# The end of a decoder step on one core: rows of two held expert blocks normalised apart and scattered over the output, in place of three blocks whose rows are fetched back into the tiles

## The reference

```python
def rmsnorm(x, g):
    xf = x.astype(jnp.float32)
    inv = lax.rsqrt(jnp.mean(xf * xf, axis=-1, keepdims=True) + EPS)
    return (xf * inv * g.astype(jnp.float32)).astype(x.dtype)
...
    def run_block(args):
        tok, w, e = args
        xb = h[tok]
        a = jax.nn.silu(xb @ w1[e]) * (xb @ w3[e])
        return ((a @ w2[e]).astype(jnp.float32) * w[:, None]).astype(h.dtype)
...
    h2 = rmsnorm(x, g_ffn).reshape(B * L, D_MODEL)
    x = x + hier_moe(h2, w_grp, w_exp, w1, w3, w2).reshape(B, L, D_MODEL)
...
    y_prompt = rmsnorm(yp, g_final)
    y_sample = rmsnorm(ys, g_final)
```

## Time and profile before

| | us |
|---|---|
| median of 3 runs | 1014.09 |
| profiled execution | 1009.91 |
| its span, first to last instruction | 1008.2 |
| PE busy in the span | 957.0 |
| last product of block 31 on PE ends | 980.3 |
| last scaled half tile on DVE ends | 1005.0 |

### The profile page before, as it was taken

One profiled execution on the slowest core, in us unless ns is written; L12 is line 12 of the kernel. 1 busy time (PEld: TensorE's weight loads), 2 busy tenths in 40 slices (PEclk: granted clock), 3 DMA queues, 4 the chain that ended last, 5 costly groups with the idle time before them and its releaser, 6 DMA issues. The chain is left out here.

```text
span 1008.2 us, 16747 instructions
## 1 busy us (share of the span) xinstructions
PE 957.0 (95%) x5480; PEld 834.8 (83%) x5481; DVE 814.8 (81%) x1873; ACT 440.3 (44%) x736; POOL 221.5 (22%) x236
## 2 busy tenths in 40 slices
PE   6999999999999999999999999969999999999980
PEld 6998898988989889898886888858888888888870
DVE  5977877878778787787878666589999999999985
ACT  6621122121221212212114112148988988988964
POOL 0001210022100212002111110031443443444332
PEclk9999999999999999999999999979999999999995
DMA  9411106121151211611127432389999999999956
GB/s 309 160 37 59 34 31 187 32 64 32 33 186 32 64 33 33 186 32 63 54 98 248 152 142 103 112 329 407 395 393 393 392 398 387 394 395 384 364 208 248
DMA packets 77190, 191.62 MB, mean 190 GB/s; under 512 B 13808, under 2 KB 49948, under 8 KB 64691
## 3 DMA queue, kind: packets, MB, share of 16 engines
q1 hardware_dynamic: 62219, 159.10, 41.9%
q0 software_dynamic: 14752, 31.03, 10.2%
q10 hardware_dynamic: 144, 0.52, 0.2%
HBM read 172.70 MB, written 38.68 MB: 210 GB/s over the span
## 5 line engine op out<-in xcount | busy, mean ns | idle before, releaser
L1422 DVE TENSOR_TENSOR w_lo<-w,w_hi 128x1024 fp32r<-128x1024 f32 x128 | 150.5, 1217 | 0.3
L845 ACT ACTIVATE w_hi<-w 128x1024 fp32r<-128x1024 f32 x128 | 129.5, 1068 | 3.4 <-PE bank L959 3.4
L957 PE MATMUL bank<-w_hi,xT_hi 128*128 128x512 f32 x256 | 102.8, 401 | 2.4 <-issue 2.3
L2178 PE MATMUL bank<-wvg_hi,hT_hi 128*128 128x512 f32 x256 | 104.0, 406 | 0.0
L2178 PE MATMUL bank<-wvg_lo,hT_hi 128*128 128x512 f32 x256 | 101.1, 395 | 0.0
L2178 PE MATMUL bank<-wvg_hi,hT_lo 128*128 128x512 f32 x256 | 100.7, 394 | 0.0
L959 PE MATMUL bank<-w_hi,xT_lo 128*128 128x512 f32 x256 | 100.1, 391 | 0.0
L958 PE MATMUL bank<-w_lo,xT_hi 128*128 128x512 f32 x256 | 99.8, 390 | 0.0
L2581 POOL TENSOR_TENSOR mixed<-onorm,pgate 128x256 f32<-128x256 f32 x36 | 28.5, 792 | 322.2 <-DVE onorm L2353 322.2
L1981 ACT ACTIVATE v<-bank 128x256 fp32r<-128x256 f32 x32 | 12.2, 383 | 195.3 <-PE bank L2179 195.3
L957 PE MATMUL bank<-hT_hi,wuqk_hi 128*128 128x344 f32 x288 | 93.5, 325 | 0.1
(11 more groups left out here) (335 smaller groups left out, 2485.0 us busy)
## 6 DMA issues: line engine op xcount, KB each, us to landing
w<-in_w_dram SPq DMA_DIRECT2D x96, 1024.0 KB
raw<-in_w_in_dram SPq DMA_DIRECT2D x57, 256.0 KB, 3.2
mixed_d<-mixed POOLq DMA_DIRECT2D x32, 128.0 KB, 2.1
sample_state<-in_state_ret_dram SPq DMA_DIRECT2D x16, 256.0 KB, 3.4
out_dram<-sample_state SPq DMA_DIRECT2D x16, 256.0 KB, 3.8
mixed_in<-mixed_d SPq DMA_DIRECT2D x8, 512.0 KB, 4.3
x_again<-in_x_prompt_dram SPq DMA_DIRECT2D x8, 512.0 KB, 3.5
h_d<-h POOLq DMA_DIRECT2D x8, 512.0 KB, 3.0
```

What stands on the lines that cost most here:

```text
L845: act.activation(hi, whole_w, ACT.Copy).then_inc(S["up_hi"], 1)
L957: pe.matmul(out, lhs[0], rhs[0], start=first, stop=False)
L1422: dve.tensor_tensor(lo, whole_w, hi, ALU.subtract).then_inc(S["up_lo"], 1)
L2178: g = pe.matmul(gates, x[xi], wvg[wi][:, 1:3, k, :], start=first, stop=last)
```

## The change

- HELD is 2: blocks 30 and 31. Block 29 is scattered with adding, as the others are.
- SP loads all eight prompt tiles after `sum_out`. Their rows are normalised whole as they are then, without the held blocks, and stored to the output.
- POOL still writes held rows back to `sum_d`, but with `idx_sample`, in which all prompt rows lie out of bounds: only rows of sample tokens are written. Then SP loads the sample parts.
- The held rows themselves are two further entries of ORDER ("block"): squared, scaled in place in `xg`, and scattered by POOL over `y_prompt` (rows of sample tokens out of bounds) once all eight tile stores have landed.
- SP stores the samples last and waits for the scatters.
- `rows_of_held` is gone. The small tables `idx_sample` and `same_row` are made on DVE in step 2 of the loop. ACT loads the table for the root inside block 31, between the gate's sigmoid and the copy of the turned rows.
- The block of engine programs is opened with `no_gpsimd_drain=True`.

```diff
-HELD = 3
+HELD = 2
...
-        block = ctx.enter_context(nc.Block())
+        block = ctx.enter_context(nc.Block(no_gpsimd_drain=True))
...
-        AGAIN = (CH, 0, 1)
-        OVER = tuple(t for t in range(CH) if t not in AGAIN)
-        ORDER = (CH, 0, 2, 1, 3, 4, 5, 6, 7)
-        NORM_GROUPS = ((0, 2), (2, 4), (4, 6), (6, 9))
+        SUMMED = tuple(("tile", t) for t in range(CH))
+        ROWS_OF_BLOCK = tuple(("block", b) for b in range(NE - HELD, NE))
+        ORDER = (*SUMMED, *ROWS_OF_BLOCK, ("samples", 0))
+        SAMPLES = len(ORDER) - 1
+        NORM_GROUPS = ((0, 3), (3, 5), (5, 8), (8, len(ORDER)))
...
             for i in range(2):
                 sp.wait_ge(sum_out[i], SUMS[i])
-            for t in OVER:
+            for t in range(CH):
                 sp.dma_start(fin[:, t, :], sum_d[t * P:(t + 1) * P, :]).then_inc(rows_in[t], 16)
...
             sp.wait_ge(z_out, 16 * HELD)
             sp.dma_start(fin_s[:, :], in_parts(sum_d[SEQ:NTOK, :])).then_inc(rows_in[CH], 16)
-            for t in (0, 1):
-                sp.dma_start(fin[:, t, :], sum_d[t * P:(t + 1) * P, :]).then_inc(rows_in[t], 16)
-            for n, t in enumerate(ORDER):
-                dst = y_prompt[0, t * P:(t + 1) * P, :] if t < CH else in_parts(y_sample.rearrange("b o d -> (b o) d"))
-                for half in halves_of(n):
-                    sp.wait_ge(S["y_done"], after(n + 1 + half.start // 512))
-                    sp.dma_start(dst[:, half], tile_of(n)[:, half]).then_inc(y_out, 16)
-            sp.wait_ge(y_out, 16 * (NT + 1))
+            for t in range(CH):
+                sp.wait_ge(S["y_done"], after(t + 1))
+                sp.dma_start(y_prompt[0, t * P:(t + 1) * P, :], fin[:, t, :]).then_inc(y_out, 16)
+            sp.wait_ge(y_out, 16 * CH)
+            sp.wait_ge(S["y_done"], after(SAMPLES + 1))
+            sp.dma_start(in_parts(y_sample.rearrange("b o d -> (b o) d")), fin_s[:, :]).then_inc(y_out, 16)
+            sp.wait_ge(y_out, 16 * (CH + 1))
+            sp.wait_ge(z_out, 16 * 2 * HELD)
...
                         down_high(b, s % SLOTS, uses(s, g), q)
                     sigmoid(b, s % 2)
+                    sqrt_next()
                     a_high(b, s % 2)
...
                     gate(b, s % 2)
+                    many.append(spill_count(dve))
                     a_low(b, s % 2)
...
+                if isinstance(b, int) and b == 2:
+                    sample_slots()
+                    same_rows()
...
+            def sample_slots():
+
+                rows = idx_tok[:, NE - HELD:NE]
+                st.do(dve.tensor_scalar(idx_past[:, :], rows, float(SEQ), 4096.0, ALU.is_lt, ALU.mult))
+                dve.tensor_tensor(idx_sample[:, :], idx_past[:, :], rows, ALU.add).then_inc(S["rows_known"], 1)
...
-            for kind, n in TAIL:
-                if kind == "norm":
-                    a, b = NORM_GROUPS[n]
-                    dve.wait_ge(S["root_done"], after(ROOT3 + n + 1))
-                    do(rsqrt_columns(steps, dve, *(small[:, at + a:at + b] for at in (SS, MS, RS, TX))))
-                else:
+            for g, (a, b) in enumerate(NORM_GROUPS):
+                do(rsqrt_columns(steps, dve, *mean_root(g)))
+                if a == CH:
+                    dve.wait_ge(z_out, 16 * HELD)
+                for n in range(a, b):
                     scale_rows(n)
...
-            for t in OVER:
+            for t in range(CH):
                 pool.wait_ge(rows_in[t], 32)
+            pool.wait_ge(S["rows_known"], after(1))
             for i, b in enumerate(range(NE - HELD, NE)):
                 pool.wait_ge(S["z_done"], after(i + 1))
-                pool.indirect_dma_start(out=sum_d, out_offset=indexed(idx_tok[:, b:b + 1]),
+                pool.indirect_dma_start(out=sum_d, out_offset=indexed(idx_sample[:, i:i + 1]),
                                         in_=xg[b % SLOTS][:, :], in_offset=None,
                                         bounds_check=last_row, oob_is_err=False).then_inc(z_out, 16)
...
-            pool.wait_ge(S["rows_known"], after(1))
-            pool.wait_ge(z_out, 16 * HELD)
-            for t in OVER:
-                landed, count = held_in(t)
-                pool.wait_ge(landed, count - 16)
-                pool.indirect_dma_start(out=fin[:, t, :], out_offset=None, in_=sum_d,
-                                        in_offset=indexed(row_held[:, t:t + 1]),
-                                        bounds_check=last_row, oob_is_err=False).then_inc(landed, 16)
+            pool.wait_ge(y_out, 16 * CH)
+            for n, (kind, b) in enumerate(ORDER):
+                if kind == "block":
+                    pool.wait_ge(S["y_done"], after(n + 1))
+                    pool.indirect_dma_start(out=y_prompt[0], out_offset=indexed(idx_tok[:, b:b + 1]),
+                                            in_=xg[b % SLOTS][:, :], in_offset=None,
+                                            bounds_check=last_prompt, oob_is_err=False).then_inc(z_out, 16)
```

More of the change, by code:

```diff
@@ L359, in step_kernel @@
         most = rc.place("most", [P, 1], F32)
[L360 to L363, removed]
+        idx_sample = rc.place("idx_sample", [P, HELD], I32)
+        idx_past = rc.place("idx_past", [P, HELD], I32)
         assert rc.at <= whole.end
@@ L618, in down_piece, with spill_count, spilled @@
             return w2t[s][at], high_of_down(b)[:, 2 * q:2 * q + 2, :], w2_lo[s][at]
-        def spilled(eng, step, build=None, end=None):
+        def spill_count(eng):
             eng.wait_ge(S["spill_known"], after(1))
-            many = eng.value_load(spill[0:1, 2 * SPILL:2 * SPILL + 1], min_val=0, max_val=SPILL)
-            with eng.If(many > 0):
+            return eng.value_load(spill[0:1, 2 * SPILL:2 * SPILL + 1], min_val=0, max_val=SPILL)
+        def spilled(eng, step, build=None, end=None, many=None):
+            with eng.If((spill_count(eng) if many is None else many) > 0):
                 if build is not None:
@@ L880, in y_out_of_psum, with sqrt_next @@
                                    scale=slot_w[:, bass.ds(b, 1)]).then_inc(S["y_ev"], 1)
+            def sqrt_next():
+                act.activation(small[:, EPSC + 1:EPSC + 2], small[:, EPSC:EPSC + 1], ACT.Sqrt)
             def y_stored(b, s, g):
@@ L933, in more, with tiles_reloaded @@
                 y_out_of_psum(b, 0)
[L935 to L941, removed]
-                else:
[L943 to L947, removed]
+            def tiles_reloaded():
+                act.wait_ge(gains_in, GAINS + 16 * CH)
+                sqrt_next()
+            spilled(act, more, held_read, tiles_reloaded)
+            for n, (kind, i) in enumerate(ORDER):
+                if kind == "tile":
+                    act.wait_ge(rows_in[i], 32)
+                elif kind == "block":
+                    act.wait_ge(S["z_done"], after(i - (NE - HELD) + 1))
+                else:
+                    act.wait_ge(rows_in[CH], 48)
+                act.wait_ge(S["sq_done"], after(SQ3 + n))
+                act.activation(junk_f[rows_of(n), 0:tile_of(n).shape[1]], tile_of(n), ACT.Square, scale=D ** -0.5,
+                               accum_out=norm_col(SSF, n)).then_inc(S["sq_done"], 1)
+                if n == SAMPLES:
                     act.wait_ge(S["l_mm"], after(NT + 1))
-                    act.activation(small[0:SR, SS:SS + 1], banks[4][0:SR, 0:1], ACT.Copy).then_inc(S["sq_done"], 1)
+                    act.activation(norm_col(SSF, n), banks[4][0:SR, 0:1], ACT.Copy).then_inc(S["sq_done"], 1)
                 for a, b in NORM_GROUPS:
                     if b == n + 1:
-                        act.wait_ge(S["sq_done"], after(squares_before(b)))
-                        root_of_means(act, a, b).then_inc(S["root_done"], 1)
+                        act.wait_ge(S["sq_done"], after(SQ3 + b + (n == SAMPLES)))
+                        act.activation(small[:, MSF + a:MSF + b], small[:, SSF + a:SSF + b], ACT.Sqrt,
+                                       bias=small[:, EPSC:EPSC + 1]).then_inc(S["root_done"], 1)
         def three(pe, out, lhs, rhs, first, last):
@@ L1587, in more, with mean_root @@
                     down_low(b, 0, q)
[L1589 to L1606 removed]
+            spilled(dve, more, spill_list, many=many[0])
+            def mean_root(g):
+                a, b = NORM_GROUPS[g]
+                dve.wait_ge(S["root_done"], after(ROOT3 + g + 1))
+                return (small[:, at + a:at + b] for at in (SSF, MSF, RSF, TXF))
+            def scale_rows(n):
+                dve.scalar_tensor_tensor(out=tile_of(n), in0=tile_of(n), scalar=norm_col(RSF, n), in1=gain_of(n),
+                                         op0=ALU.mult, op1=ALU.mult).then_inc(S["y_done"], 1)
+            dve.wait_ge(gains_in, GAINS)
+            for g, (a, b) in enumerate(NORM_GROUPS):
[3 more added lines that the diff above has]
+                for n in range(a, b):
                     scale_rows(n)
```

79 lines of the change are left out of this document (32 added, 47 removed).

## The result

The changed kernel takes 1015.86 us (median of 14 runs) against 1012.7 us for the kernel before (14 runs): a ratio of 1.0042, 95% interval 1.0032 to 1.0052, or 3.2 to 5.3 us slower. The forecast was 1016.9 us and slower. The time came 1.0 us under it: the two medians differ by 3.2 us, 0.4 more than the forecast's 2.8, and the median of the kernel before, which the forecast had from three runs, stands 1.4 us lower in fourteen. The ratio puts the loss higher, at 4.3 us; it goes by the fast runs alone, which leaves out two of the kernel before (1541.94 and 2470.76 us).

A forecast was written before the change was run, and what follows sets the result against it. The prediction took the end to hang on DMA hand-overs, then DVE; links summed on the profile's clock to 1011.0 against 1008.2, 2.8 us later, making the median 1014.09 into 1016.9 us, range 1014.4 to 1019.4.

The forecast's parts named there:

- the samples' writes: POOL's two writes before the samples' load: second starts 1.31 us after the first and lands 2.56 us later, at 994.0.
- the balance that the forecast drew: Six gathers and two late loads leave the path; loads start 8.3 us later, a POOL hand-over adds over 4 us.
- the landing of the adding scatter: Block 29's scatter, ahead of the tile loads: taken to land in 4.3 us, at 974.5 (972.8 to 979.0).
- the bound from above: For block 29's scatter landing: 5.4 us, block 28's same instruction with other traffic bringing the window to 109 GB/s.
- the early landing: Rival: block 29's scatter lands like a write, 2.6 us in place of 4.3; 1015.2 us, no measurable change; chance 0.24.
- The lower end of the range: For the whole kernel: 1014.4 us, an early landing of block 29's scatter with a short write for the samples.
- DVE, the end before, is off the path: At the stores: DVE scales the eighth tile by 1001.5, the DMA comes to it at 1004.5; cover 3 us.
- No gate: Rival: the stores' wait for the samples' writes costs nothing, stores start as tiles are scaled; 1011.7 us; chance 0.05.
- Slower DMA: Rival: bare loads and stores move at 365 GB/s, each 1.0 us longer; 1018.9 us; chance 0.07.
- Drain: Rival: POOL still drains behind the second output scatter, ending the span 5 us later; 1022 us; chance 0.04.
- the four small instructions of step 2: On DVE in the loop, about 0.2 us each: can push PE by 0 to 0.8 us, taken as 0.2.

The follow-up runs named there:

- old_end_held2: The kernel before with two blocks held in place of three, its end unchanged: 1021.11 us, ratio 1.0084 to the kernel before.
- new_end_held3: The changed kernel with three blocks held in place of two, nothing else: 1010.32 us, ratio 0.9983 to the kernel before.
- plain_scatter29: The changed kernel with block 29's scatter overwriting rows of the sums in place of adding: 1014.22 us in a single run.
- gains_first: The changed kernel with the samples' gains loaded ahead of the tile loads: 1018.53 us, ratio 1.0059 to the kernel before.
- stores_ungated: The changed kernel with three stores ahead of SP's wait for the samples' writes: 1014.57 us, ratio 1.0023 to the kernel before.
- gains_and_stores: The changed kernel with gains loaded first and three stores ahead of the wait for the samples' writes: 1014.04 us, ratio 1.0018 to the kernel before.
- drain_back: The changed kernel with POOL's drain at the end put back: 1020.7 us, ratio 1.0090 to the kernel before.
- held3_best: The changed kernel with three held blocks, gains first, samples' load after six stores, samples a norm group: 1006.82 us, ratio 0.9940 to before.

## Why the prediction was right, and where it wasn't

The links on the profile's clock, in us:

| link | forecast | measured |
|---|---|---|
| block 29's result to its scatter | 0.8 | 0.8 |
| scatter to the first load | 4.3 | 5.2 |
| first load to the last tile landed | 14.7 | 14.9 |
| last tile to the samples' first write | 0.9 | 0.9 |
| samples' writes to SP's release | 3.9 | 3.4 |
| samples' load to first store | 0.6 | 0.6 |
| first store to the first scatter over the output | 12.0 | 12.2 |
| that scatter to the landing of the second | 3.9 | 3.8 |
| landing to the end | 0.4 | 0.5 |
| sum | 41.4 | 42.3 |

**The mechanism** was right: the chain runs through every link of the sum, the stores wait for the samples' writes, and the end hangs on two scatters behind the last store. *old_end_held2* and *new_end_held3* show the balance that the forecast drew: a shorter end, given back by the later loads. How near the sum came is in part chance: the scatter's landing (0.9 us too short) and the samples' writes (0.5 too long) partly cancel.

**Mis-sized: the landing of the adding scatter.** The sum took 4.3 us, between a write and a landing under traffic; it is 5.1 on an idle DMA, close to the bound from above, and *plain_scatter29* shows that the addition, not the traffic, makes the difference. So the early landing, the rival with the most chance, was further off than I thought, and most of its gain was given back in the one run that forced it.

**The samples' writes** land 2.1 us after the start of the second (993.73 to 995.84), not 2.56. The Trainium skill, "DMA: Bandwidth & Descriptors" (Anatomy of one DMA), gives a POOL-issued DMA about 2.0 us fixed plus its bytes. For these writes, which carry hardly a row, the trace agrees; for the adding scatter with its 5.1 us it doesn't, since its at most 128 rows (0.524 MB) move in 1.3 us at 397 GB/s (an estimate from the window at 998). The lower end of the range, 1014.4, comes from no row: the early landing's 1015.2 with writes as short as measured is 1014.8.

**The step that failed: "DVE, the end before, is off the path", with 3 us of cover.** I had DVE free once its additions were done and its roots and squares there. They were, but its first scaling also waits for the samples' gains, which I had costed at nothing: eight small loads on SP behind eight large ones, landed at 993.1, after the last tile. At the first store, 996.43, one tile was scaled and the second just about, where I had three or more waiting; the eighth was scaled at 1005.2, not by 1001.5. So there was no cover; DVE and DMA ended level, and that DVE ended no later is luck. *gains_first* shows that this cost the end nothing (12.2 us from first store to scatter with DVE early or late), and *stores_ungated* that it bounds as soon as the gate opens.

**The rivals.** No gate: SP's list held, and *gains_and_stores* prices it at 4.2 us of stretch once DVE is early (43.6 to 39.4); with DVE late it was 0.6. Slower DMA: the full windows show 397 to 410 GB/s, so the stores took what the sum gave them; the rule of 358 GB/s in the Trainium skill, same page (Where 436 GB/s comes from), does not hold here either. Drain: it is gone, and *drain_back* prices it at 5.4 us, where the rival had 5.

**The remainder.** The links give 3.5 us over the kernel before, the ratio 3.2 to 5.3. What lies ahead of block 29's result moved by 1.3 us in the profiles; of it the four small instructions of step 2, costed at 0.2, make 0.25. From the first block's result to the sixth's it takes 47.17 us in both kernels with the old end, which lack them there, and 47.41 to 47.47 in the nine with the new. The rest varies from run to run.

## What to carry to other kernels

When work is moved from the end to an earlier hand-over, first ask what that hand-over delays: here one adding scatter more ahead of the loads cost 5 to 8 us, and the rebuilt end earned 2 to 4 (in the old end with two held, without the 2 us of its gathers). List every wait of the first instruction of a group, small loads too, and put a small load that is ready early ahead of the large ones in its queue. Two waits that end level hide each other, so open them together: singly they gave 1.2 us worse and 0.6 better here, together 2.9 better, in one profile each.

## What the hardware showed that I had not expected

- POOL's issue of an indirect write without adding takes 0.97 to 1.02 us with DVE idle. Where it starts while DVE is scaling a 128 x 1024 tile, it ends 0.85 to 0.89 us after that tile, and so takes 1.17 to 1.98 us (1.17, 1.54 and 1.85 in *held3_best*, 1.67 in *gains_first*, 1.92 in *plain_scatter29*, 1.98 in *drain_back*). Where the scaling had begun only 0.06 us earlier, it is short (1.00 in *stores_ungated*), and with DVE held still it is 1.00 again. DVE's additions from PSUM (L1497), under way at 979.81 in the kernel before, did not lengthen it (1.01 us).
- The same scatter lands in 5.1 us if it adds and in 2.8 if it writes, with nothing else on the DMA.
- POOL's drain at the program's end lasts until some 7 us after its last indirect issue (6.9 and 7.2); in *drain_back* it ends 5.5 us after SP, which waits for the landing of POOL's last scatter, was done.
